# Expert outputs scattered as two rounded parts, with one buffer of fetched tokens and reordered queues

## Time and profile before

| what | value |
|---|---|
| median of 3 runs | 3825.28 us |
| profiled execution | 3822.87 us |
| its span on the core | 3821.1 us |
| mean granted TensorE clock over the span | 0.847 |
| expert stage, first rounding to the end of the last scatter | 1323.6 to 2489.6 us of the span, 1166.0 us |
| TensorE busy in that stage | 1153.05 us |
| VectorE, ScalarE busy in that stage | 1033.22 us, 859.83 us |
| DMA busy share in that stage | 0.90, 335 GB/s |

### The profile page before, as it was taken

One profiled execution on the slowest core, in us unless ns is written; L12 is line 12 of the kernel. 1 busy time (PEld: TensorE's weight loads), 2 busy tenths in 40 slices (PEclk: granted clock), 3 DMA queues, 4 the chain that ended last, 5 costly groups with the idle time before them and its releaser, 6 DMA issues. The chain is left out here.

```text
span 3821.1 us, 47370 instructions
## 1 busy us (share of the span) xinstructions
PE 3138.3 (82%) x17428; PEld 2566.4 (67%) x17429; DVE 2243.2 (59%) x3232; ACT 1570.7 (41%) x1975; POOL 143.6 (4%) x175
## 2 busy tenths in 40 slices
PE   7689999888875799999999999938446987735788
PEld 2358888656665688888888888728224987723788
DVE  1235555444444599889889898735344655443555
ACT  0024444311122377777777777613111443210343
POOL 0022323000000000000000000000000000000000
PEclk9789999977877699999999999969556998855899
DMA  7350100111132499999999999633001543200443
GB/s 256 98 80 24 44 23 1 36 33 33 33 121 98 187 356 354 347 344 357 340 351 355 341 358 345 229 112 110 7 1 51 169 157 108 83 0 7 149 148 104
DMA packets 225356, 606.58 MB, mean 159 GB/s; under 512 B 21858, under 2 KB 79769, under 8 KB 225049
## 3 DMA queue, kind: packets, MB, share of 16 engines
q1 hardware_dynamic: 219996, 598.46, 44.4%
q10 hardware_dynamic: 5181, 5.76, 0.5%
HBM read 599.78 MB, written 4.39 MB: 158 GB/s over the span
## 5 line engine op out<-in xcount | busy, mean ns | idle before, releaser
L1688 DVE TENSOR_TENSOR moe_raw_r<-moe_raw,moe_hi 128x2048 fp32r<-128x2048 f32 x320 | 720.4, 2285 | 14.6 <-ACT moe_hi L1626 14.6
L1626 ACT ACTIVATE moe_hi<-moe_raw 128x2048 fp32r<-128x2048 f32 x320 | 599.9, 1907 | 99.8 <-PE banks L1550 99.6
L321 PE MATMUL banks<-ff_xs,ff_hi 128*128 128x272 f32 (+1 forms) x1024 | 298.0, 291 | 70.5 <-DVE ff_raw_r L337 61.1
L1550 PE MATMUL banks<-moe_raw_r,moe_xs 128*128 128x512 f32 x1024 | 344.5, 419 | 0.0
L322 PE MATMUL banks<-ff_xs,ff_hi 128*128 128x272 f32 (+1 forms) x1024 | 296.3, 289 | 0.0
L323 PE MATMUL banks<-ff_xs,ff_raw_r 128*128 128x272 f32 (+1 forms) x1024 | 295.3, 288 | 0.0
L1550 PE MATMUL banks<-moe_hi,moe_xs 128*128 128x512 f32 x772 | 281.7, 449 | 6.7 <-DVE moe_raw_r L1688 5.3
L321 PEld LDWEIGHTS banks<-ff_xs,ff_hi 128*128 128x128 f32 x1024 | 196.9, 192 | 74.2 <-issue 62.3
L1550 PEld LDWEIGHTS banks<-moe_raw_r,moe_xs 128*128 128x128 f32 x1024 | 210.2, 205 | 53.1
L323 PEld LDWEIGHTS banks<-ff_xs,ff_raw_r 128*128 128x128 f32 x1024 | 197.1, 192 | 0.0
L322 PEld LDWEIGHTS banks<-ff_xs,ff_hi 128*128 128x128 f32 x1024 | 197.0, 192 | 0.0
(11 more groups left out here) (476 smaller groups left out, 6503.1 us busy)
## 6 DMA issues: line engine op xcount, KB each, us to landing
moe_raw<-in_w_gu SPq DMA_DIRECT2D x256, 1024.0 KB, 9.4
moe_raw<-in_w_down SPq DMA_DIRECT2D x128, 1024.0 KB, 10.6
ff_raw<-in_w_ff SPq DMA_DIRECT2D x128, 512.0 KB, 3.8
ring_mod<-in_w_mod SPq DMA_DIRECT2D x12, 2048.0 KB, 8.5
wq<-in_w_in SPq DMA_DIRECT2D x32, 512.0 KB, 4.2
ring_att<-in_w_in SPq DMA_DIRECT2D x32, 512.0 KB, 3.7
ring_att<-in_w_in SPq DMA_DIRECT2D x32, 448.0 KB, 3.5
wh<-in_w_in SPq DMA_DIRECT2D x10, 1024.0 KB, 8.5
```

Of the source, the lines that this page charges most:

```text
L321: pe.matmul(ps[m][:, :n], w_hi, x_hi, start=(k == 0), stop=False)
L1550: ins = pe.matmul(ps[pair(e) + c][:, :], x[:, k, :], w[:, k * D + c * 512:k * D + c * 512 + 512], start=first, stop=last)
L1626: act.activation(hi[n % HI_SLOTS][:, :], raw[n % UNITS][:, :], ACT.Copy).then_inc(his, 1)
L1688: dve.tensor_tensor(rest[n % UNITS][:, :], raw[n % UNITS][:, :], hi[n % HI_SLOTS][:, :].bitcast(F32), ALU.subtract).then_inc(los, 1)
```

```diff
-        pickT = sb("pickT", [2 * SLOTS, LAT])
+        pickT = sb("pickT", [2 * SLOTS, LAT], FR)
...
-        xs = sb("moe_xs", [P, 2, KT, 2 * SLOTS], FR)
+        xs = sb("moe_xs", [P, KT, 2 * SLOTS], FR)
...
-        y_sb, acs = both_types(ctx, nc, "y_tok", [P, KT, 2 * SLOTS])
-        y = y_sb[:, :, :].rearrange("p k n -> p (k n)")
+        acs = sb("acs", [P, KT, 2 * SLOTS], FR)
+        y_hi = acs[:, :, :].rearrange("p k n -> p (k n)")
+        y_lo = sb("y_lo", [P, D], FR)
+        y_parts = (y_hi, y_lo)
...
                 def scatter(e):
-                    pe.wait_ge(y_out, e + 1)
+                    pe.wait_ge(y_rest, e + 1)
                     for t in range(2):
-                        for c in range(2):
-                            ins = pe.matmul(ps[4 + 2 * t + c][:, :], pickT[:, t * P:(t + 1) * P], y[:, c * 512:(c + 1) * 512],
-                                            start=False, stop=(e == NEXP - 1))
+                        for part in range(2):
+                            for c in range(2):
+                                ins = pe.matmul(ps[4 + 2 * t + c][:, :], pickT[:, t * P:(t + 1) * P],
+                                                y_parts[part][:, c * 512:(c + 1) * 512],
+                                                start=False, stop=(e == NEXP - 1 and part == 1))
...
                     nxt = e + 1 < NEXP
+                    turn(e, 1)
                     if nxt:
                         pe.wait_ge(x_out, e + 2)
-                        for q in range(2):
-                            unit("g", e + 1, q)
-                    turn(e, 1)
-                    if nxt:
-                        for q in range(2, 4):
+                        for q in range(4):
                             unit("g", e + 1, q)
...
                         for q in range(4):
                             unit("u", e + 1, q)
-                            if q == 1:
+                            if q == 2:
                                 scatter(e)
                                 slots_in(e + 1)
...
+                    if nxt:
+                        rounded(g0)
                     if e:
                         results(e - 1)
                     if nxt:
-                        for q in range(3):
-                            rounded(g0 + q)
+                        rounded(g0 + 1)
+                        rounded(g0 + 2)
                     slots_out(e)
                     if nxt:
                         rounded(g0 + 3)
                     rounded(d0)
                     out("u", e)
+                    rounded(d0 + 1)
                     if nxt:
                         x_of(e + 1)
-                    rounded(d0 + 1)
+                    sigmoid(e, 0)
                     rounded(d0 + 2)
-                    sigmoid(e, 0)
                     rounded(d0 + 3)
+                    if nxt:
+                        rounded(u0)
                     sigmoid(e, 1)
                     if nxt:
+                        rounded(u0 + 1)
                         out("g", e + 1)
-                        for q in range(4):
-                            rounded(u0 + q)
+                        rounded(u0 + 2)
+                        rounded(u0 + 3)
...
+                def y_second(e):
+                    dve.wait_ge(y_out, e + 1)
+                    dve.scalar_tensor_tensor(y_lo[:, :].rearrange("p (b n) -> p b n", b=2), ps.all[:, pair(e):pair(e) + 2, :],
+                                             gslot[:, 0:1], y_hi.bitcast(F32).rearrange("p (b n) -> p b n", b=2),
+                                             ALU.mult, ALU.subtract).then_inc(y_rest, 1)
...
+                    if e:
+                        y_second(e - 1)
                     if nxt:
-                        lo(g0)
+                        lo(g0, g0 + 1)
                         if e + 2 < NEXP:
                             dve.wait_ge(slots, e + 1)
                             hot_of(e + 2)
-                        lo(g0 + 1, g0 + 2, g0 + 3)
+                        lo(g0 + 2, g0 + 3)
                     lo(d0)
                     act_first(e, 0)
                     lo(d0 + 1)
                     act_second(e, 0)
+                    lo(d0 + 2)
                     act_first(e, 1)
-                    lo(d0 + 2)
+                    lo(d0 + 3)
                     act_second(e, 1)
-                    lo(d0 + 3)
                     if nxt:
                         lo(u0, u0 + 1, u0 + 2, u0 + 3)
+                y_second(NEXP - 1)
```

More of the change, by code:

```diff
@@ L1531, in experts @@
         names = ("hot gath x_out his los used gu_out turned t_free glu clip sig prod act_hi act_ready slots s_out y_out "
-                 "scat")
+                 "y_rest scat")
         with stage(nc, names, held=loaded) as (block, hot, gath, x_out, his, los, used, gu_out, turned, t_free, glu, clip,
-                                               sig, prod, act_hi, act_ready, slots, s_out, y_out, scat):
+                                               sig, prod, act_hi, act_ready, slots, s_out, y_out, y_rest, scat):
             @block.sync
@@ L1544, in unit @@
                     n = place[ph, e, q]
-                    x = (acs if ph == "d" else xs[:, e % 2])[:, 2 * q:2 * q + 2, :]
+                    x = (acs if ph == "d" else xs[:, :, :])[:, 2 * q:2 * q + 2, :]
                     pe.wait_ge(los, n + 1)
@@ L1629, in x_of @@
                     act.wait_ge(gath, e + 1)
-                    act.activation(xs[:, e % 2], gathered(pair(e)), ACT.Copy).then_inc(x_out, 1)
+                    act.activation(xs[:, :, :], gathered(pair(e)), ACT.Copy).then_inc(x_out, 1)
                 def out(ph, e):
@@ L1644, in results @@
                     act.wait_ge(s_out, e + 1)
-                    act.activation(y.rearrange("p (b n) -> p b n", b=2), ps.all[:, pair(e):pair(e) + 2, :], ACT.Copy,
+                    act.activation(y_hi.rearrange("p (b n) -> p b n", b=2), ps.all[:, pair(e):pair(e) + 2, :], ACT.Copy,
                                    scale=gslot[:, 0:1]).then_inc(y_out, 1)
@@ L1775, in experts @@
         over_names = ("o_hot o_gath o_x o_used o_his o_los o_gu_out o_turned o_t_free o_glu o_sig o_act_ready o_gcol o_gt_mm "
-                      "o_gt_out o_y_out o_sc_mm o_added o_act_v")
+                      "o_gt_out o_y_out o_y_rest o_sc_mm o_added o_act_v")
         with stage(nc, over_names + " " + over_loads) as (block, hot, gath, x_out, used, his, los, gu_out, turned, t_free, glu,
-                                                          sig, act_ready, gcol, gt_mm, gt_out, y_out, sc_mm, added, act_v,
+                                                          sig, act_ready, gcol, gt_mm, gt_out, y_out, y_rest, sc_mm, added, act_v,
                                                           *loads):
@@ L1825, in body @@
                     for u in range(8):
-                        products(i, u, ps[u // 2][:, :], xs[:, 0, u % 2 * 4:u % 2 * 4 + 4, :])
+                        products(i, u, ps[u // 2][:, :], xs[:, u % 2 * 4:u % 2 * 4 + 4, :])
                         if u == 3:
@@ L1838, in body @@
                         products(i, u, ps[6 + u % 2][:, :], acs[:, (u - 8) // 2 * 4:(u - 8) // 2 * 4 + 4, :])
-                    pe.wait_ge(y_out, i + 1)
+                    pe.wait_ge(y_rest, i + 1)
                     for r in range(4):
@@ L1842, in body @@
                             k = 2 * r + m
-                            ins = pe.matmul(ps[4 + r][:, m * LAT:(m + 1) * LAT], y[:, k * P:(k + 1) * P], pickT[:, :],
-                                            start=True, stop=True)
+                            for part in range(2):
+                                ins = pe.matmul(ps[r][:, m * LAT:(m + 1) * LAT], y_parts[part][:, k * P:(k + 1) * P],
+                                                pickT[:, :], start=(part == 0), stop=(part == 1))
                         ins.then_inc(sc_mm, 1)
@@ L1898, in body @@
                     assert v.n == ACT_STEPS
+                    dve.wait_ge(y_out, i + 1)
+                    dve.scalar_tensor_tensor(y_lo[:, :].rearrange("p (b n) -> p b n", b=2), ps.all[:, 6:8, :],
+                                             gslot[:, 0:1], y_hi.bitcast(F32).rearrange("p (b n) -> p b n", b=2),
+                                             ALU.mult, ALU.subtract).then_inc(y_rest, 1)
                     dve.wait_ge(added, i * 4 + 4)
@@ L1902, in body @@
                         dve.tensor_tensor(yT[:, 2 * r:2 * r + 2, :], yT[:, 2 * r:2 * r + 2, :],
-                                          ps[4 + r][:, :].rearrange("p (k t) -> p k t", k=2), ALU.add).then_inc(added, 1)
+                                          ps[r][:, :].rearrange("p (k t) -> p k t", k=2), ALU.add).then_inc(added, 1)
                 further(dve, body)
@@ L1925, in body @@
                     act.wait_ge(gath, i + 1)
-                    act.activation(xs[:, 0], gathered(0), ACT.Copy).then_inc(x_out, 1)
```

(5 more changed lines are left out.)

## The result

| | before | changed |
|---|---|---|
| median | 3823.9 us (6 runs, 3819.61 to 3828.51) | 3837.55 us (6 runs, 3834.47 to 3844.34) |
| ratio | | 1.004 (95% interval 1.0027 to 1.0053) |
| profiled execution | 3822.87 us | 3843.85 us |
| mean of 28 periods in the middle of the stage | 36.17 us | 36.71 us |

The change costs 13.7 us, where +14 was forecast.

What follows compares the result with a forecast made beforehand. TensorE's own sequence was taken to bound the stage. (0.14 + 0.3 + 0.05) x 30 = +14.7 us, less 0.3 and rounding, gave +14 on 3825.3: 3839 us, range 3790 to 3860 us.

Steps and rivals of the forecast that it cites:

- TensorE's sequence bounds the stage: Stage of slices 14 to 26: TensorE hardly waits, so every microsecond added to or taken from its sequence counts once a period.
- The scatter, -1.56 us: TensorE's scatter: eight matmuls at the units' rate take 1.87 us instead of 3.43, gaining 1.56 us a period.
- The second turn, +1.70 us: Moved directly behind the first turn, it runs at half clock, 3.40 us instead of 1.70, costing 1.70 us a period.
- Both low stretches become 3.4 us longer: TensorE's time at clock 0.50 after the fetch starts grows to about 10.2 and 6.8 us in the two period kinds.
- a rival: Cheaper turn: clock returns sooner or drops no longer than today, leaving the scatter's gain; -39 us, 3786 us; chance 0.18.
- The chain through `y_second`, +0.3 us: VectorE's chain from g0 takes 19.1 us against TensorE's ten units of 18.7; TensorE waits 0.3 us a period at the scatter.
- it just fits: 0: At d2: the activation's second half is ready 9.0 us after g0, TensorE arrives after 9.3; no wait.
- Adding the terms: Turn and scatter +0.14, chain +0.3 and mix +0.05 us a period were added and multiplied by 30.
- The single buffer, +0: `xs` with one buffer: its copy waits for the fetch, when units reading the old contents are over; cost 0.
- The page's rule: Mid-kernel clock drops come from idle gaps; by it the turn's move costs nothing, leaving the scatter's gain alone.
- The mix, +0.05: Longer periods ask for more of the long kind, now 6 in 10; +0.05 us a period, bounds 0 and 0.3.
- The periods that I named, 35.6 and 37.1 us: Expected lengths of the two period kinds in the changed profile, alongside low stretches of 6.8 and 10.2 us.

Runs made afterwards that it cites:

- no_rest: Changed kernel without `y_second`; the scatter's second four matmuls read the rounded part again. Measured 3843.02 us, ratio 1.0051.
- y_twice: Changed kernel with VectorE's read of the expert's output in PSUM doubled by an unused maximum ahead of each `y_second`. Measured 3832.69 us, ratio 1.0022.
- split_late: split_alone with one edit: scatter and slots come one unit later, after the third u unit. Measured 3787.8 us, ratio 0.9914.
- x_single: Kernel before with one buffer of fetched tokens instead of two, nothing else. Measured 3823.94 us, ratio 1.0002.
- split_alone: Kernel before's engine orders, plus the change's fp32r scatter, single `xs` buffer and `y_second` at the head of VectorE's period. Measured 3878.19 us, ratio 1.0164.
- turn_back: Changed kernel with the second turn put back in its old place behind g1. Measured 3765.85 us, ratio 0.9852.
- full_clock: no_long_run with VectorE reordered: d1's split ahead of the activation's first half, d2's split inside it. Measured 3753.33 us, ratio 0.981.
- no_long_run: Changed kernel with TensorE's fetch and turns in pieces between units, tokens copied in halves, `y_second` ahead of the last u split. Measured 3787.27 us, ratio 0.9902.

## Why the prediction was right, and where its steps were not

The sign, the size and the mean period came out: +14 us forecast, +13.7 measured; +0.49 us a period forecast, +0.54 measured. The terms behind the sum did not hold so well. Two errors cancelled, so that the sum came out this close is luck.

- **TensorE's sequence bounds the stage.** Right for the kernel before. After the change TensorE waits for VectorE in every period.
- **The scatter, -1.56 us.** Measured 3.43 - 1.97 = 1.46: right.
- **The second turn, +1.70 us.** The step that failed is "Both low stretches become 3.4 us longer" in every period. In the slow kind the term is right: the turn runs at half clock (6.83 us for two), and the low stretch grows from 6.8 to 10.2 us. With the measured waits that gives 36.80 - 1.46 + 1.70 + 0.70 = 37.74 us for the 37.80 seen. But a quarter of the periods, which I did not foresee as a kind, have no drop at all. Low clock rose from 5.49 to 7.68 us a period, 2.19 us, and at half speed that is worth 1.1 us, not 1.7. I had listed the warm first two periods as evidence for a rival and did not ask whether they could recur.
- **The chain through `y_second`, +0.3 us.** Mis-sized: 0.56 us at the scatter in both kinds, of which `y_second` itself is as priced (1.28 us, 1.20 from start to start, for 1.25). At d2, where I wrote "it just fits: 0", TensorE waits 0.48 us in the warm kind and 0.14 in the slow one: 2103.31 follows 2102.70 by 0.61 where 0.47 is the pace. Together 0.7 to 1.05, about 0.8 on average.
- **The sum again**: -1.46 + 1.1 + 0.8 = +0.44; the 0.1 that is left may be the starts after a wait (0.57 instead of 0.47 us for the first pair).
- **Adding the terms.** For the mean period the runs refute this most clearly. no_rest takes 0.8 us of waits away and gains 0.13; y_twice adds 1.1 us of wait and gains 0.4. split_late takes 1.8 us of wait away and gains 2.6. Within periods of one kind the terms do add: 37.0 and 37.8 us in no_rest and the changed kernel, 33.4 and 34.6 in the changed kernel and y_twice. What the sum lacks is the mix: with each wait the number of periods of each kind changed. That a wait shifts where the drop falls, and so decides whether a period has one, is my reading of it.
- **The single buffer, +0.** Right (x_single).
- **The page's rule.** I set the rule of the Trainium skill ("TensorE: Matmul & The Clock Gate", "Why this matters for your kernels"), that gaps of idleness lower the clock, against the rows, and followed the rows. no_rest, at 0.87 and busy for 1024.16 of 1024.16 us, shows that the drops behind the fetch need no gap. But the rule has its place in this kernel too: split_alone agrees with it, where the clock falls after 14 of 30 waits of 2.8 us at the scatter. My sum for an order with such waits would lack that cost.
- **The mix, +0.05.** Right in direction: 6 in 10 slow periods became 3 in 4; wrong in what the other quarter is. The periods that I named, 35.6 and 37.1 us, were seen in no_rest alone, where `y_second` and its waits are left out; with the wait of 0.3 us my own terms give 37.2, not 37.1, for the longer one.

In short, from turn_back: with the turn in its old place the changed kernel is 72 us faster, so the move of the turn costs the 58 us that the rest of the change gains and 14 us more.

What stays open: which drops occur in a given period. Slow and warm periods of the changed kernel do the same work in the same order, and no run here fixes by itself where the narrow work falls. And why three kernels share 34.1 us was not tested by an experiment of its own; their DMA engines are at 0.96 to 0.97, but full_clock goes on to 33.65 us with them at 0.99.

## What to carry to other kernels

Where TensorE alternates between wide and narrow products, look at the granted clock inside one period, and keep narrow work in short pieces with wide products between: the place of one turn was worth 2.5 us of 36.7 here, and all the pieces of full_clock 3.1. Sort the periods by their low time before comparing two kernels: a wait adds within one kind. For the mean don't add up a wait and a clock term, but run the pair, because a wait removed can come back as low clock and a wait added can vanish. And when an edit moves the result of one engine later, place the consumer by the producer's chain: one unit of cover ahead of the scatter was worth 90 us, 56 of it as wait and the rest as clock.

## What the runs showed of the hardware

- TensorE's clock fell while it was never idle: no_rest is busy for 1024.16 of 1024.16 us and has the lowest mean clock, 0.87; no_long_run is busy for 927.13 of 970.24 us, idle in short waits, and has 1.00.
- It also fell after idleness: in split_alone behind 14 of 30 waits of 2.8 us, for 3.41 us each (1488.59 to 1492.00).
- Narrow matmuls in one piece did not always lower it: 7.06 us of them ran at 1.00 (2046.60 to 2053.66), and in the next period the clock fell 3.5 us into the same piece (2080.02 to 2083.50).
- A float32 matmul of 128x512 takes 3.43 / 4 = 0.86 us, an fp32r one in a run of its kind 0.23 us, so two fp32r products for one float32 product still save nearly half.
- More work on another engine need not cost time: y_twice took 3832.69 us against 3837.55 for the changed kernel, with 1.1 us more of VectorE's work and of TensorE's wait a period.
- The DMA engines ran at a share of 0.99 and 372 GB/s over 942 us in full_clock; the kernel before held 346 GB/s. The faster periods had room up to there.
